# Where the small tables stand in the on-chip memory of a two-block transformer kernel

## The chip, the cores and the metric

The kernel runs on one NeuronCore of a Trainium2 chip. The metric is the device time of one execution in microseconds (us). It was run three times: 1253.51 us in the median, 1253.32 to 1254.24 us in all. A separate execution was recorded by the hardware profiler, and all rows below come from that one.

## The reference, cut to what matters

The program computes two stacks of two layers each on an input `x` of 256 tokens by 1024 features in float32. The first stack has a spatial gating unit beside an RWKV-7 time mix, then dilated attention, each followed by a gated feed-forward layer with a three-tap convolution. The second stack has block attention and a short gated convolution, each followed by a SwiGLU layer, with shifts, scales and gates computed from a condition vector.

```python
for layer in range(DEPTH):                                   # first stack
    x = x + mixer(rmsnorm(x, g)) @ w_out
    x = x + conv_glu_ffn(rmsnorm(x, ff_norm[layer]), w_up, conv_w, conv_b, w_down)
x = rmsnorm(x, final_norm)
for i in range(DEPTH):                                       # second stack
    sh_m, sc_m, g_m, sh_f, sc_f, g_f = split(silu(c) @ w_ada[i] + b_ada[i])
    x = x + g_m * mixer_2(modulate(x, norm_mix[i], sh_m, sc_m))
    x = x + g_f * swiglu(modulate(x, norm_ffn[i], sh_f, sc_f), w_gate_up[i], w_down[i])
```

Nearly all of the arithmetic is in the dense products with weights from DRAM: `w_in`, `w_qkv`, `w_up` and `w_gate_up` (1024 rows), the output matrices (1024 by 1024) and `w_down` (2816 by 1024).

## The kernel before, in words

Every float32 factor of a large product is split into a high part, rounded to the TensorE type fp32r, and a low part, the rounding's remainder. A product is then three matmuls: high by high, high by low, low by high.

**Weights.** `sync_program` loads chunks of 1 or 2 MB from DRAM into two ring buffers (`ring0`, `ring1`, 4096 columns each). Half a chunk at a time, ScalarE makes the high part (`split_hi`, L617) in one of four buffers `WHI`, and VectorE the low part (`split_lo`, L623) in one of four buffers `WLO` (2048 columns each, float32 size). TensorE takes the halves in order and gives each back through the semaphore `w_used`.

**The four kinds of stream on TensorE.** With NK = 8 blocks of 128 rows to sum over:

- `pe_tile` (L1080 to L1082) keeps a 128x128 block of weights in the array and sends 256 columns (the 256 tokens) of the activations `HT0` or `HT1`, three matmuls per block. In the profile `HT0` is `hhi`/`hlo` and `HT1` is `ghi`/`glo`.
- `pe_rows` (L1095 to L1097) and `pe_first` (L847 to L849) do the reverse: a block of the activations is in the array, and 256 columns of `WHI`/`WLO` are sent. In `pe_first` for the feed-forward layers those are two runs of 128 columns, 1024 columns apart; in `pe_rows` one run of 256.
- `pe_sum_part` (L1109) has a block of `YT` (`yhi`/`ylo`) in the array and sends 512 columns of `WHI`/`WLO`.

In every matmul row of the profile the names after the arrow are the operand that is sent and then the one in the array; LDWEIGHTS rows (PEld) are the loading of the latter.

**Places in the memory.** Buffers are handed out in the order of the `sb` and `part` calls, from the bottom of each partition upwards, each at the next free place: first the ring, `WHI`, `WLO`, `X`, `XN` and `YT` (131,072 bytes together in each partition), then the small tables `CT` (constants, 2120 columns), `COL` (776), `MODC` (64), `SM` (192) and `ONE_R32` (128), together 3280 columns or 13,120 bytes, and then `AHI`/`ALO` (2 KB each) and one region that `RW`, `HT0`, `SV` and later `HT1`, `AR`, `GBT`, `ACC` and others use in turn. `TMPS` and the others in an `ExitStack` that is closed at once share their place with what follows.

**Order of the work.** It is written out by hand for each engine (`OD`, `MO`, `walk`, `ADA_AT`, the bank plan for the eight PSUM banks); engines meet only in semaphores. No table of costs looks at an address.

Of the kernel before, what the change touches and what calls it, by code (L numbers as in the profile page):

```python
# [9 lines left out]
F32R = mybir.dt.float32r  # L10
# [28 lines left out]
NC = C_Y64 + 6 * 64  # L39
# [417 lines left out]
def program(nc, A, consts, out):  # L457
    with ExitStack() as ctx:
        def sb(name, cols, dt=F32, rows=128):
            return ctx.enter_context(nc.sbuf_tensor(name, [rows, cols], dt))  # L460
# [4 lines left out]
        def c3(ap, k):  # L465
            return ap.rearrange("p (k n) -> p k n", k=k)
# [4 lines left out]
        def rep(ap, n):  # L471
            return ap.unsqueeze(1).to_broadcast([ap.shape[0], n, ap.shape[1]])
# [10 lines left out]
            return flat(ap)[0].partition_broadcast(128)  # L483


        ring = [sb(f"ring{i}", SLOT) for i in range(NS)]
        WHI = [sb(f"whi{i}", HALF, F32R)[:, :] for i in range(NB)]
        WLO = [sb(f"wlo{i}", HALF, F32R)[:, :] for i in range(NB)]
        X = c3(sb("x", 2 * D)[:, :], 2)
        XN = c3(sb("xn", 2 * D)[:, :], 2)  # L490
        YT = [c3(sb(f"y{i}", NK * T, F32R)[:, :], NK) for i in ("hi", "lo")]
        CT = sb("consts_sb", NC)
        COL = sb("cols", 6 * 128 + 8)
        MODC = sb("modc", 2 * 4 * 8)
        SM = sb("small", 192)
        ONE_R32 = sb("one_r", 128, F32R)[:, :]
        NORM = ExitStack()
        TMPS = [part(NORM, f"tmp{i}", 512)[:, :] for i in range(2)]
        NORM.close()
# [17 lines left out]
        PS = [ctx.enter_context(nc.psum_tensor(f"ps{i}", [128, 512], F32)) for i in range(8)]  # L517
        ident = CT[:, C_ID:C_ID + 128]
        ones = CT[:, C_ONE:C_ONE + 128]

# [9 lines left out]
        def area(kib, n):  # L530
            return AR[:, kib * 256:kib * 256 + n]
# [10 lines left out]
        def ps_of(key):  # L542
            return PS[bank_of[key][0]]

        def bank_sem(key):
            return bank_sems[bank_of[key][0]]
# [131 lines left out]
        def cc(name, i=0, n=1):  # L678
            return COL[:, col[name] + i:col[name] + i + n]

        def conv_col(l, j, i):
            q = l * 3 + j
            s = (1 + q // 2) * 128 + q % 2 * 44 + i
            return COL[:, s:s + 1]

        small_at = [0]

        def sm(n):
            s = small_at[0]
            small_at[0] += n  # L690
            assert small_at[0] <= 192
            return SM[:, s:s + n]

# [60 lines left out]
        def mask(c):  # L754
            return rep(CT[:, c:c + 128].bitcast(U32), 4)

        def mask64(c, n):
            return rep(CT[:, c:c + 64].bitcast(U32), n)

# [4 lines left out]
        GB = [[GBT[:, 1024 * (2 * l + f):1024 * (2 * l + f) + 1024] for f in range(2)] for l in range(2)]  # L764
        modc = MODC[:, :].rearrange("p (l q k) -> p l q k", l=2, q=4)
        AW = c3(area(16, 4096), NK)
# [30 lines left out]
        def pe_column(e, t):  # L797
            ps = opened(e, ("col", t))
            e.wait_ge(S[f"rows{t}"], 16 * len(row_parts[t]))
            k = n_rows[t]  # L800
            e.transpose(ps[:, 0:k], PRS[t][0:k, :], CT[0:k, C_ID:C_ID + k]).then_inc(S["col_turned"], 1)

        COL_ORDER = (6, 0, 1, 2, 3, 4, 5)

        def dve_column(e, t):
            e.wait_ge(S["col_turned"], COL_ORDER.index(t) + 1)
            e.tensor_copy(COL[:, t * 128:t * 128 + n_rows[t]],
                          ps_of(("col", t))[:, 0:n_rows[t]]).then_inc(bank_sem(("col", t)), 1)
# [395 lines left out]
        def sync_program(e):  # L1204
# [8 lines left out]
            for dst, src in ((W2A[0:64, :], A["ev_w2"][0]), (W2A[64:128, :], A["ev_a2"][0]), (G2, A["ev_g2"][0])):  # L1213
                e.dma_start(dst, src).then_inc(S["lora_in"], 16)
            e.dma_start(CT[:, C_ONE:], consts[:, C_ONE:]).then_inc(S["consts_in"], 16)
            w.made = 1
# [113 lines left out]
        def scalar_program(e):  # L1330
# [187 lines left out]

            e.activation(ONE_R32, ones, ACT.Copy).then_inc(S["one_in"], 1)
            act_ffn(e, w, 0, 1, ("u", 1))  # L1520
# [171 lines left out]
        def gate_no(n):  # L1692
            return n // 6 * 2 + n % 2 + 1
# [999 lines left out]
        def pe_ada_sums(e, blocks):  # L2693

            for n in blocks:
# [5 lines left out]
                e.wait_ge(S["ada_lo"], gate_no(n))  # L2701
                e.matmul(ps[:, :], ONE_R32, AHI, start=True, stop=False)
                e.matmul(ps[:, :], ONE_R32, ALO, start=False, stop=True).then_inc(S["ada_mm"], 1)

# [60 lines left out]
```

## Time and profile before

| | |
|---|---|
| median of three runs | 1253.51 us |
| span of the profiled execution | 1253.0 us |
| TensorE busy (PE) | 1230.9 us, 9987 matmuls |
| TensorE weight loads (PEld) | 1147.4 us |
| VectorE busy (DVE) | 933.6 us |
| ScalarE busy (ACT) | 703.9 us |
| mean DMA rate | 211 GB/s |
| mean granted TensorE clock | 0.999 |

The span of the profiled execution is 0.5 us below the median of the runs. A busy TensorE is one that has a matmul somewhere in its pipeline: consecutive matmuls overlap in the record (the one that takes 281 ns is followed by the next after less than half of that), so the distance from start to start, and not the duration of a row, tells how fast a stream goes.

### The profile page before, as it was taken

To read this page: it belongs to the slowest core of one execution; us is meant where nothing else is said; L and a number is where in the kernel's file an instruction comes from. 1 tells how busy PE (TensorE), PEld (TensorE's weight loads), DVE (VectorE), ACT (ScalarE), POOL (GpSimd) and SP (SyncE) were. 2 spreads that over 40 slices of the span, in tenths; PEclk is the share of its full clock that TensorE was granted. 3 is DMA by queue.
4 is the path that set the end of the run, shared out by engine and by line. 5 is a ranking of instruction groups with operands and counts; after the bars stand their busy time and mean duration, and the time that the engine had idled before them with its cause. 6 is when DMAs were issued, how large, how long until landed. Compare 5 with 4: busy or idle time off the path is not lost.

```text
span 1253.0 us, 23639 instructions
## 1 busy us (share of the span) xinstructions
PE 1230.9 (98%) x9987; PEld 1147.4 (92%) x9987; DVE 933.6 (75%) x1260; ACT 703.9 (56%) x1032; POOL 20.1 (2%) x31
## 2 busy tenths in 40 slices
PE   6999999999999999999999999999999999999998
PEld 6999889999999879999988998999998998999997
DVE  5888369888758777999987566899976666677453
ACT  6843477555555767666657556634445554643432
POOL 0002000000000000000000000000000000000000
PEclk9999999999999999999999999999999999999999
DMA  9450277776567256689653534899965356675540
GB/s 322 168 201 4 69 247 246 250 238 229 193 220 257 105 170 234 217 291 319 249 201 119 194 130 148 290 360 351 343 234 202 136 204 200 236 250 188 202 169 34
DMA packets 163683, 263.78 MB, mean 211 GB/s; under 512 B 5677, under 2 KB 98041, under 8 KB 163578
## 3 DMA queue, kind: packets, MB, share of 16 engines
q1 hardware_dynamic: 160586, 259.54, 60.3%
q10 hardware_dynamic: 2992, 2.72, 0.7%
q8 instruction: 79, 1.29, 0.4%
q14 instruction: 26, 0.21, 0.1%
HBM read 261.17 MB, written 1.05 MB: 209 GB/s over the span
## 4 chain that ended last, share of the span: by engine, by line
PE 97%; DVE 1%; ACT 1%; DMA 1%; issue 1%; SPq 0%; DVEq 0%; ACTq 0%
PE ps L1109 26%; PE ps L1080 17%; PE ps L1082 16%; PE ps L1081 16%; PE ps L847 2%; PE ps L848 2%; PE ps L849 2%; PE ps L1095 2%; PE ps L1097 2%; PE ps L1096 2%; PE ps L2397 2%; PE ps L827 1%; DMA ring<-in_ev_w_in_dram 1%; PE ps L2406 1%; PE ps L2597 1%
## 5 line engine op out<-in xcount | busy, mean ns | idle before, releaser
L623 DVE TENSOR_TENSOR wlo<-ring,whi 128x2048 fp32r<-128x2048 f32 x194 | 443.3, 2289 | 97.6 <-ACT whi L617 97.6
L1080 PE MATMUL ps<-ghi,whi 128*128 128x256 f32 x1600 | 449.0, 281 | 0.0
L1081 PE MATMUL ps<-glo,whi 128*128 128x256 f32 x1600 | 446.8, 279 | 0.0
L1082 PE MATMUL ps<-ghi,wlo 128*128 128x256 f32 x1600 | 446.5, 279 | 0.0
L617 ACT ACTIVATE whi<-ring 128x2048 fp32r<-128x2048 f32 x194 | 370.4, 1913 | 96.7 <-PE ps L1109 69.7
L1080 PEld LDWEIGHTS ps<-ghi,whi 128*128 128x128 f32 x1600 | 300.4, 188 | 2.0 <-DVE wlo L623 0.6
L1081 PEld LDWEIGHTS ps<-glo,whi 128*128 128x128 f32 x1600 | 299.7, 187 | 0.8
L1082 PEld LDWEIGHTS ps<-ghi,wlo 128*128 128x128 f32 x1600 | 300.4, 188 | 0.0
L1109 PE MATMUL ps<-whi,yhi 128*128 128x512 f32 x480 | 159.7, 396 | 0.7 <-DVE ylo L1996 0.7
L1109 PE MATMUL ps<-wlo,yhi 128*128 128x512 f32 x480 | 156.7, 390 | 0.0
L1109 PE MATMUL ps<-whi,ylo 128*128 128x512 f32 x480 | 156.6, 390 | 0.0
L1109 PEld LDWEIGHTS ps<-whi,ylo 128*128 128x128 f32 x480 | 90.1, 188 | 19.2
L1109 PEld LDWEIGHTS ps<-wlo,yhi 128*128 128x128 f32 x480 | 90.1, 188 | 18.9
L1109 PEld LDWEIGHTS ps<-whi,yhi 128*128 128x128 f32 x480 | 88.2, 188 | 20.3 <-issue 2.4
L2218 DVE SCALAR_TENSOR_TENSOR acc<-arena,small,acc 128x512 f32<-128x512 f32 x126 | 94.7, 751 | 6.4 <-DMA arena<-in_w_ada_dram 2.5
L2255 DVE SCALAR_TENSOR_TENSOR arena<-arena,cols 128x254 f32<-128x254 f32 (+1 forms) x176 | 73.9, 479 | 14.7 <-ACT arena L1770 14.2
L1774 ACT ACTIVATE arena<-ps 128x256 f32<-128x256 f32 x44 | 16.9, 384 | 111.8 <-PE ps L1082 111.8
L2270 DVE TENSOR_TENSOR ylo<-arena,yhi 128x256 fp32r<-128x256 f32 x88 | 37.1, 422 | 47.6 <-ACT yhi L1787 47.4
L847 PE MATMUL ps<-whi,ghi 128*128 128x256 f32 x224 | 63.5, 283 | 4.0 <-DVE glo L993 4.0
L1768 ACT ACTIVATE arena<-ps 128x512 f32<-128x512 f32 x44 | 26.3, 599 | 67.1 <-PE ps L1082 65.5
L849 PE MATMUL ps<-whi,glo 128*128 128x256 f32 x224 | 62.6, 279 | 0.0
L848 PE MATMUL ps<-wlo,ghi 128*128 128x256 f32 x224 | 62.5, 279 | 0.0
(314 smaller groups left out, 1575.0 us busy)
## 6 DMA issues: line engine op xcount, KB each, us to landing
arena<-in_w_ada_dram SPq DMA_DIRECT2D x48, 1024.0 KB, 6.0
ring<-in_ff_w_up_dram SPq DMA_DIRECT2D x44, 1024.0 KB, 7.6
ring<-in_w_gate_up_dram SPq DMA_DIRECT2D x44, 1024.0 KB, 7.5
ring<-in_ff_w_down_dram SPq DMA_DIRECT2D x10, 2048.0 KB, 7.9
ring<-in_w_down_dram SPq DMA_DIRECT2D x10, 2048.0 KB, 7.8
ring<-in_od_w_qkv_dram SPq DMA_DIRECT2D x6, 2048.0 KB, 8.6
ring<-in_w_qkv_dram SPq DMA_DIRECT2D x6, 2048.0 KB, 7.9
ring<-in_w_in_dram SPq DMA_DIRECT2D x6, 2048.0 KB, 8.1
```

Of the source, the lines that this page charges most:

```text
L617: e.activation(shaped(WHI[i % NB], k), v, ACT.Copy).then_inc(S["w_hi"], 1)
L623: e.tensor_tensor(shaped(WLO[i % NB], k), v, shaped(WHI[i % NB], k).bitcast(F32), ALU.subtract).then_inc(S["w_lo"], 1)
L847: e.matmul(o, h[0][:, c, t], wh, start=c == 0, stop=False)
L848: e.matmul(o, h[0][:, c, t], wl, start=False, stop=False)
L849: x = e.matmul(o, h[1][:, c, t], wh, start=False, stop=c == NK - 1)
L1080: e.matmul(o, wh, h[0][:, k, :], start=k == 0, stop=False)
L1081: e.matmul(o, wh, h[1][:, k, :], start=False, stop=False)
L1082: x = e.matmul(o, wl, h[0][:, k, :], start=False, stop=k == NK - 1)
L1109: x = e.matmul(ps[:, :], YT[l][:, src_k + i, t], w[r][:, i, 512 * h:512 * h + 512], start=first, stop=last)
L2218: e.scalar_tensor_tensor(a, AW[:, k, :], SC[:, k:k + 1], a, ALU.mult, ALU.add).then_inc(S["ada_acc"], 1)
L2255: e.scalar_tensor_tensor(t[a][:, lag:256], z[:, 256 * a:256 * a + 256 - lag], conv_col(f, 2 - lag, a * NF + p), t[a][:, lag:256], ALU.mult ...
L2270: e.tensor_tensor(YT[1][:, p % 8, :], tg[r], YT[0][:, p % 8, :].bitcast(F32), ALU.subtract).then_inc(S["y_lo"], 1)
```

## The change

The five small tables are allocated first, ahead of the ring, and an unused buffer `even` of 16 columns (64 bytes) follows them. All else is as before: the same instructions in the same order, the same semaphores, the same sizes.

```diff
+        CT = sb("consts_sb", NC)
+        COL = sb("cols", 6 * 128 + 8)
+        MODC = sb("modc", 2 * 4 * 8)
+        SM = sb("small", 192)
+        ONE_R32 = sb("one_r", 128, F32R)[:, :]
+        sb("even", 16)
         ring = [sb(f"ring{i}", SLOT) for i in range(NS)]
         WHI = [sb(f"whi{i}", HALF, F32R)[:, :] for i in range(NB)]
         WLO = [sb(f"wlo{i}", HALF, F32R)[:, :] for i in range(NB)]
         X = c3(sb("x", 2 * D)[:, :], 2)
         XN = c3(sb("xn", 2 * D)[:, :], 2)
         YT = [c3(sb(f"y{i}", NK * T, F32R)[:, :], NK) for i in ("hi", "lo")]
-        CT = sb("consts_sb", NC)
-        COL = sb("cols", 6 * 128 + 8)
-        MODC = sb("modc", 2 * 4 * 8)
-        SM = sb("small", 192)
-        ONE_R32 = sb("one_r", 128, F32R)[:, :]
```

The allocator's first free place is byte 1152 of each partition, which 13,120 + 64 bytes of tables and filling bring to 14,336, seven times 2048. So the remainders of the start addresses by 2048 bytes are:

| buffers | before | after |
|---|---|---|
| `ring`, `WHI`, `WLO`, `X`, `XN`, `YT` | 1152 | 0 |
| `CT` | 1152 | 1152 |
| `AHI`, `ALO`, `HT0`, `HT1`, `AR`, `GBT` and the rest | 1984 | 0 |

## Rows read from the trace of the kernel before

**Rows 1.** The page, section 1: busy time of TensorE.

```profile
PE 1230.9 (98%) x9987; PEld 1147.4 (92%) x9987; DVE 933.6 (75%) x1260; ACT 703.9 (56%) x1032; POOL 20.1 (2%) x31
```

**Rows 2.** Waits of TensorE, the longest: who waited for whom, us in total, times, longest.

```profile
PE ps L801 <- DMA pre<-in_ev_norm_dram: 5.1, 1, 5.1
```

**Rows 3.** Groups by line: name, shapes, count | busy us, mean ns | idle before.

```profile
L1080 PE MATMUL ps<-ghi,whi 128*128 128x256 f32 x1600 | 449.0, 281 | 0.0
...
L1109 PE MATMUL ps<-whi,yhi 128*128 128x512 f32 x480 | 159.7, 396 | 0.7 <-DVE ylo L1996 0.7
...
L847 PE MATMUL ps<-whi,ghi 128*128 128x256 f32 x224 | 63.5, 283 | 4.0 <-DVE glo L993 4.0
...
L1095 PE MATMUL ps<-whi,ghi 128*128 128x256 f32 x160 | 45.7, 286 | 0.1
...
L1080 PE MATMUL ps<-hhi,whi 128*128 128x256 f32 x144 | 42.5, 295 | 2.2 <-issue 2.2
...
L1095 PE MATMUL ps<-whi,hhi 128*128 128x256 f32 x32 | 9.1, 286 | 0.0
```

**Rows 4.** Timeline of TensorE, 600 to 604 us (`pe_tile`): start, duration.

```profile
599.85 0.28 PE L1080 MATMUL ps<-ghi,whi 128*128 128x256 f32 x1
...
600.20 0.28 PE L1080 MATMUL ps<-ghi,whi 128*128 128x256 f32 x1
...
600.55 0.28 PE L1080 MATMUL ps<-ghi,whi 128*128 128x256 f32 x1
...
603.73 0.28 PE L1080 MATMUL ps<-ghi,whi 128*128 128x256 f32 x1
```

**Rows 5.** The chain that ended last, 51 to 64 us: start, us, piece.

```profile
51.93 0.12 PE ps L1097
...
62.59 0.11 PE ps L1080
...
62.93 0.44 PE ps L2329 x4
63.37 0.12 PE ps L1080
...
63.72 0.12 PE ps L1080
```

**Rows 6.** Timeline of TensorE, 781 to 785 us (`pe_first`).

```profile
781.23 0.28 PE L847 MATMUL ps<-whi,ghi 128*128 128x256 f32 x1
...
782.25 0.28 PE L847 MATMUL ps<-whi,ghi 128*128 128x256 f32 x1
...
782.95 0.28 PE L847 MATMUL ps<-whi,ghi 128*128 128x256 f32 x1
...
784.72 0.28 PE L847 MATMUL ps<-whi,ghi 128*128 128x256 f32 x1
```

**Rows 7.** The chain, 220 to 227 us (`pe_sum_part`).

```profile
219.90 7.25 PE ps L1109 x32
```

**Rows 8.** Windows: length, busy (count) by engine, granted clock, DMA share, GB/s.

```profile
411.00:413.00 2.00, 2.00 (x20) 2.00 (x19) 1.90 (x5) 0.00 (x0) 0.00 (x0) 1.00 0.00 0
600.00:604.00 4.00, 4.00 (x37) 4.00 (x36) 4.00 (x3) 1.79 (x1) 0.00 (x0) 1.00 1.00 397
697.00:702.00 5.00, 5.00 (x45) 5.00 (x44) 3.47 (x5) 2.33 (x5) 0.00 (x0) 1.00 0.02 5
```

**Rows 9.** The chain, 0 to 60 us: first load, and a product before TensorE speeds up.

```profile
1.65 7.38 DMA ring<-in_ev_w_in_dram
...
20.48 0.21 PE ps L1081
```

**Rows 10.** DMA issues: transfer, queue, count, size, median us to landing.

```profile
arena<-in_w_ada_dram SPq DMA_DIRECT2D x48, 1024.0 KB, 6.0
ring<-in_ff_w_up_dram SPq DMA_DIRECT2D x44, 1024.0 KB, 7.6
```

## The prediction

> **What bounds the kernel now.** The page's busy times come first. TensorE is busy for 1230.9 us of a span of 1253.0 us, VectorE for 933.6 and ScalarE for 703.9 [rows 1]. So TensorE stands still for 22.1 us in all, of which the longest single wait is the 5.1 us before its first instruction, for a small load [rows 2]. No faster load, copy or VectorE operation can be worth more than those 22 us. What else can move the time is the pace of the products themselves, so the second thing to read is which products there are and how far apart they start.
>
> The groups by line give the products of 256 sent columns: each row stands for one of three lines of the same count. They are 3 x (1600 + 144) = 5232 in `pe_tile` and 3 x (224 + 160 + 32) = 1248 in `pe_first` and `pe_rows`, 6480 together. Those of 512 sent columns are 3 x 480 = 1440 [rows 3]. The mean durations there (281, 396 ns) overlap, so the pace has to come from the starts.
>
> - `pe_tile` at 600 us: from 599.85 to 603.73 us lie 33 starts, 117.6 ns each [rows 4].
> - The same line at 52 to 62 us: from 51.93 to 62.59 us lie 94 starts, 113.4 ns each [rows 5].
> - `pe_first` has both in one stream: 9 starts from 781.23 to 782.25 us are 113.3 ns apart, 15 from 782.95 to 784.72 us are 118.0 [rows 6].
> - `pe_sum_part`: 32 in 7.25 us, 226.6 ns each, twice the short pace of 256 columns [rows 7].
>
> So products of 256 columns have exactly two paces, 4.4 ns apart. Going along the timeline I count about 840 at the short pace and 5,600 at the long one (a few are irregular). Nearly all of `pe_tile` goes at the long pace (the short one only around 52 to 63, 87 to 93, 485 and 676 to 682 us), and about half of the 1248 others go at the short one. The total is 6480 x 0.118 + 1440 x 0.227 = 765 + 327 = 1092 us, 87% of the span: this is where an address could count.
>
> **What the change removes, adds and moves.** No instruction, DMA, wait or semaphore is added, removed or reordered on any engine or queue; `even` is never touched. What changes is start addresses. The large operands start at remainder 1152 (the weights, `YT`, ring) or 1984 (`HT0`, `HT1`, arena) of 2048 bytes before, and at 0 after. Each of the following effects is therefore a price per access.
>
> *Crossing a 2 KB boundary.* In `pe_tile` a product sends 1024 bytes starting at 1984 + 1024k. For even k that crosses a multiple of 2048, for odd k it does not. Successive triples of one k start 0.35 us apart in both cases (599.85, 600.20, 600.55) [rows 4]. In the stretch at the short pace 31 triples fit 10.66 us, with no room for a dear and a cheap kind [rows 5]. Aligned, no such product crosses; by these rows that is worth 0, at most the 0.01 us resolution of a row over a triple, and the long averages make it far less.
>
> *The remainder of the sent operand.* At 51.93 us TensorE goes without a pause from sending weights (remainder 128 by 256) to sending `hhi` (remainder 192 by 256), and the pace stays 113 ns. After four small matmuls at 62.93 us the same line with the same `hhi` is at 117 ns (63.37 to 63.72) [rows 5]. In [rows 6] the pace changes in mid-stream, with the operands' remainders unchanged. So before the change the pace is something the pipeline falls into, kept until something disturbs it, and the address of the operand does not choose it. I value this at 0. Its bounds: if alignment chose the short pace for all, 5600 x 4.4 ns = 24.6 us are saved; if it chose the long one for all, 840 x 4.4 ns = 3.7 us are lost, and 6.3 us more if the 512-column products got the same step (1440 x 4.4 ns).
>
> *DMA traffic against TensorE.* The stretch at 411 us goes at the short pace with a DMA share of 0.00, the one at 697 us at the long one with 0.02 (45 products in 5.00 us with those at the edges), the one at 600 us also, with 1.00 [rows 8]. So where DMAs land has no say in the pace: 0.
>
> *DMAs themselves.* In 1.65 to 9.03 us the chain is the first 1 MB of weights [rows 9]; the ring starts off a multiple of 256 bytes and will start on one. The gain is between 0 and 1.4 us: the lower end because nothing about the transfer's pieces changes, the upper because the fastest other 1 MB load lands in 6.0 us and this one took 7.4 [rows 9, 10]. (The 6.0 us load also has longer pieces, so it overstates.) I take 0.2 us, near the lower end, since after this load ScalarE's and VectorE's work for the norm still lies before the first product. All later loads are behind TensorE's work, which is busy for all but 22.1 us.
>
> The Trainium skill, "DMA: Bandwidth & Descriptors", section "How a descriptor splits into AXI transactions", says that a piece which does not start at a multiple of 256 bytes begins with a transfer from the boundary below and pays for the unused bytes. By it a 1 KB piece off the boundary costs up to 36 beats where 32 would do, which of the 7.4 us would be 0.8 (an estimate); it speaks of reads, and the trace has no aligned ring load to test it.
>
> *VectorE and ScalarE.* They read and write the same buffers at new addresses, and are idle for 319 and 549 us [rows 1], so a small change in their pace is hidden. If it weren't, the 22.1 us of TensorE's idle time would grow; I put 0.
>
> Sum: 1253.0 - 0.2 = 1252.8 us for the profiled execution. The runs' median lies 0.5 us above that execution, so the forecast is 1253.3 us.
>
> **The rivals.**
>
> *Long pace gone (faster).* One memory serves both the load of the next block into the array and the columns that are sent; where their addresses stand to one another may decide which of the two paces a stream keeps. For it: every stream at the long pace has `HT0` or `HT1` on one side, whose remainder differs from that of the weights on the other; the 512-column products, whose two operands have the same remainder now, run at 226.6 ns, exactly twice the short pace [rows 7]. The change gives all of them one remainder. Against it: [rows 5, 6], both paces at one pair of addresses; and a 512-column product leaves more time for the load, which may be why it has one pace only. Price 24.6 us: 1228.9 us. If only some streams change over, some 10 to 14 us and 1240 us.
>
> *All overhead gone (much faster).* If what the products take beyond one column per cycle came from misaligned starts, both shapes would gain. Half of the 0.21 us that a product takes at 20.48 us, at the lower clock level [rows 9], is 0.107 us (256 columns at 2.4 GHz). Then 5600 x 10.9 + 880 x 6.7 + 1440 x 13.3 ns = 61 + 6 + 19 = 86 us go: 1167 us. Against it is that the overhead is proportional to the columns (6.7 for 256, 13.3 for 512), where a bad start would cost once.
>
> The Trainium skill, "TensorE: Matmul & The Clock Gate", section "Back-to-back issue gap", gives columns / 2.4 + 2.5 ns: 109.2 and 215.8 ns. No row reaches either; if aligned operands did, the same sum would give some 67 us, 1187 us (an estimate).
>
> *Addresses now coincide (slower).* With all remainders 0, load and sent columns start in the same place of every 2 KB, and if the two sides meet in the same part of the memory each meeting costs. It decides from the point where a stream that now goes at the short pace can no longer keep it. Then those 840 products pay 3.7 us (1257.2 us), and if the 512-column ones, which are in step already, also take the step, 6.3 us more: 1263.5 us. For it: the long pace is by far the commoner one, so it is easily fallen into. Against it: the 512-column products have equal remainders now and do not take the step.
>
> *The change does nothing at all:* 1253.5 us, in the forecast's case.
>
> **How the numbers follow.** Forecast (addresses have no say) 0.50, with its own range 1251.5 to 1254.8 us. Long pace gone 0.20, partly gone 0.07, all overhead gone 0.03. Coinciding addresses 0.20, half of it with the 512-column products. A measurement of this kernel tells about 0.2%, 2.5 us, from no change. So faster 0.30, same 0.50, slower 0.20. The range of 1227 to 1260 us takes in the forecast, both cases of a lost long pace, and the first half of the slower case; outside remain 0.03 below and about 0.10 above.
>
> **What would show it.** If I am right, starts in `pe_tile` stay 117.6 ns apart and in `pe_sum_part` 226.6, the stretches at 113 ns are about as many as now, and busy TensorE stays at 1231 us. If `pe_tile` shows 113.3 ns between starts throughout, the first rival holds; under 113, the second; if `pe_rows` around 411 us shows 118 or `pe_sum_part` over 227, the third. The first ring load landing sooner than 7.4 us, with the first product of the `lora` tile ahead of 15.4 us, would show the DMA term. What makes me wrong is a dependence on addresses that the trace of before, having only one set of them, cannot show.

## The result and the profile after

The changed kernel is slower: 1269.11 us in the median (1268.82 to 1269.93, four runs) against 1253.84 us; the ratio is 1.0122, 95% interval 1.011 to 1.0134. The span of its profiled execution is 1267.0 us, 14.0 us more than before. The forecast was 1253.3 us, and the measured time lies 9 us above the upper end of the stated range, 1260 us.

The page after, section 1, answers to [rows 1]:

```profile
PE 1245.5 (98%) x9987; PEld 1162.7 (92%) x9987; DVE 934.9 (74%) x1260; ACT 703.2 (56%) x1032; POOL 20.7 (2%) x31
```

TensorE is busy 14.6 us longer with the same 9987 matmuls, and its idle time is 21.5 us where it was 22.1. So the loss lies in the pace of the products. All line numbers after the diff are one higher. Here is the timeline of TensorE after, in `pe_tile`, which answers to [rows 4]; columns are start and duration in us:

```profile
606.76 0.28 PE L1081 MATMUL ps<-ghi,whi 128*128 128x256 f32 x1
...
610.72 0.28 PE L1081 MATMUL ps<-ghi,whi 128*128 128x256 f32 x1
```

From 606.76 to 610.72 us lie 33 starts: 120.0 ns each, where it was 117.6. The timeline where `pe_rows` ends and `pe_tile` with `hhi` begins answers to [rows 5]:

```profile
51.82 0.28 PE L1098 MATMUL ps<-whi,hlo 128*128 128x256 f32 x1
51.94 0.28 PE L1081 MATMUL ps<-hhi,whi 128*128 128x256 f32 x1
...
63.10 0.28 PE L1081 MATMUL ps<-hhi,whi 128*128 128x256 f32 x1
```

From 51.94 to 63.10 us: 93 starts, 120.0 ns. It was 113.4. `pe_first` in the third feed-forward layer, which showed both paces in [rows 6], has only 120 ns too:

```profile
789.80 0.28 PE L848 MATMUL ps<-whi,ghi 128*128 128x256 f32 x1
...
790.52 0.28 PE L848 MATMUL ps<-whi,ghi 128*128 128x256 f32 x1
```

(six starts in 0.72 us). The 512-column products are as they were in [rows 7], 24 in 5.44 us, 226.7 ns. This is the chain that ended last, after:

```profile
221.92 5.44 PE ps L1110 x24
```

Summed over all starts (each product is given the time to the next start), the 5232 products of `pe_tile` take 10.9 us more, the 672 of `pe_first` 2.1, the 576 of `pe_rows` 2.9, the 1440 of `pe_sum_part` 0.2 less, and everything else 1.7 less, of which 0.5 us is an earlier start. That is the whole of the 14.0 us. Both old paces, 113.3 and 117.8 ns, are gone and a third one, 120.0 ns, stands in their place. The 0.5 us at the start and the DMA issues answer to [rows 9, 10]:

```profile
1.65 6.92 DMA ring<-in_ev_w_in_dram
```

```profile
arena<-in_w_ada_dram SPq DMA_DIRECT2D x48, 1024.0 KB, 5.5
ring<-in_ff_w_up_dram SPq DMA_DIRECT2D x44, 1024.0 KB, 7.2
```

### The profile page after: what moved, and what is told of

Its sections match the earlier page's. It is cut to its first block, busy times and chain, and to the rows that moved or that the text cites. A ratio compares the mean times of both kernels' runs of the same rounds, so it can differ in the third digit from the quotient of the medians.

```text
span 1267.0 us, 23639 instructions
## 1 busy us (share of the span) xinstructions
PE 1245.5 (98%) x9987; PEld 1162.7 (92%) x9987; DVE 934.9 (74%) x1260; ACT 703.2 (56%) x1032; POOL 20.7 (2%) x31
## 3 DMA queue, kind: packets, MB, share of 16 engines
q10 hardware_dynamic: 2992, 2.72, 0.8%
## 4 chain that ended last, share of the span: by engine, by line
PE 97%; DVE 1%; ACT 1%; DMA 1%; issue 1%; SPq 0%; DVEq 0%; ACTq 0%
PE ps L1110 25%; PE ps L1081 17%; PE ps L1082 17%; PE ps L1083 17%; PE ps L848 2%; PE ps L850 2%; PE ps L849 2%; PE ps L1096 2%; PE ps L1098 2%; PE ps L1097 2%; PE ps L2398 2%; PE ps L828 1%; DMA ring<-in_ev_w_in_dram 1%; PE ps L2407 1%; PE ps L2598 1%
## 5 line engine op out<-in xcount | busy, mean ns | idle before, releaser
L624 DVE TENSOR_TENSOR wlo<-ring,whi 128x2048 fp32r<-128x2048 f32 x194 | 443.1, 2288 | 100.2 <-ACT whi L618 99.9
L1081 PE MATMUL ps<-ghi,whi 128*128 128x256 f32 x1600 | 454.1, 284 | 0.0
L1083 PE MATMUL ps<-ghi,wlo 128*128 128x256 f32 x1600 | 452.7, 283 | 0.0
L1082 PE MATMUL ps<-glo,whi 128*128 128x256 f32 x1600 | 452.7, 283 | 0.0
L1081 PEld LDWEIGHTS ps<-ghi,whi 128*128 128x128 f32 x1600 | 306.8, 192 | 2.0 <-issue 1.2
L1082 PEld LDWEIGHTS ps<-glo,whi 128*128 128x128 f32 x1600 | 306.9, 192 | 0.9
L1083 PEld LDWEIGHTS ps<-ghi,wlo 128*128 128x128 f32 x1600 | 306.8, 192 | 0.0
```

Source lines behind the costliest of these rows:

```text
L624: e.tensor_tensor(shaped(WLO[i % NB], k), v, shaped(WHI[i % NB], k).bitcast(F32), ALU.subtract).then_inc(S["w_lo"], 1)
L1081: e.matmul(o, wh, h[0][:, k, :], start=k == 0, stop=False)
L1082: e.matmul(o, wh, h[1][:, k, :], start=False, stop=False)
L1083: x = e.matmul(o, wl, h[0][:, k, :], start=False, stop=k == NK - 1)
```

## The experiments

In all of them no instruction changes, only the places of buffers. `sb` counts columns of 4 bytes, so 48 columns are 192 bytes. "Mean pace" is worked out from all starts between 105 and 130 ns apart (for `pe_sum_part`, under 245 ns). The difference D is the start of `HT0`/`HT1` minus the start of the weights, in bytes modulo 256.

**1. Is it the boundary or the relative position?**

```diff
-        sb("even", 16)                    # e1_no_even: all at remainder 1984, D = 0
```

> The tables stay in front, the 64-byte filling is left out: weights, YT and HT0/HT1 all start at remainder 1984 by 2048 bytes, so they are still equal to one another but at no boundary. Theory 1 (what counts is how the addresses of the two operands stand to one another): all products of 256 columns start 120.0 ns apart as after the change, about 1269 us. Theory 2 (what counts is that operands start on the 2 KB boundary): 113 and 118 ns as before the change, about 1254 us.

```diff
+        sb("even", 16)                    # e2_acts_aligned: kernel before, behind the tables; D = 128
```

> The order of before, with only the 64-byte filling behind the tables: weights and YT at remainder 1152, HT0/HT1 and the arena at 0 (896 bytes ahead by 1024). Theory 1 (relative position): not 120 ns throughout; a pace of its own, since this difference is a new one. Theory 2a (HT on the 2 KB boundary is what costs): 120 ns, 1269 us.

```diff
         YT = [c3(sb(f"y{i}", NK * T, F32R)[:, :], NK) for i in ("hi", "lo")]
+        sb("gap", 240)                    # e3_gap960: 960 bytes, D = 192
+        sb("gap", 80)                     # e4_gap320: instead, 320 bytes, D = 64
```

> The kernel after with 960 unused bytes between YT and the rest: weights at 0, HT0/HT1 at 960. Theory 1 (relative position): not 120 ns, near 113 to 118, under 1262 us. Theory 2b (weights on the 2 KB boundary are what costs): 120 ns throughout, 1269 us.

> The kernel after with 320 unused bytes between YT and the rest: weights at 0, HT0/HT1 at 320. Before the change HT stood 832 bytes behind the weights by 2048, which is 320 by 512. Theory 1, if the pattern repeats every 512 bytes or less: the two paces of before, 113.3 and 117.8 ns, with pe_tile nearly all at the longer, about 1254 us. Theory 2b (weights on the boundary cost): 120 ns, 1269 us.

Measured against before: without `even` 1270.23 us, ratio 1.0139 (1.011 to 1.0169); HT aligned alone 1265.62 us, 1.0103 (1.0073 to 1.0132); gap 960 1246.04 us, 0.9934 (0.9906 to 0.9962); gap 320 1253.56 us, 1.0003 (0.9991 to 1.0014). The timeline of the kernel without `even`, in which no large operand starts on a 2 KB boundary:

```profile
606.98 0.28 PE L1080 MATMUL ps<-ghi,whi 128*128 128x256 f32 x1
...
609.86 0.28 PE L1080 MATMUL ps<-ghi,whi 128*128 128x256 f32 x1
```

24 starts in 2.88 us are 120.0 ns. The boundary is not it. With weights on the boundary and a gap of 960, the page and the `pe_tile` pace at 598 us are these:

```profile
PE 1222.3 (98%) x9987; PEld 1139.5 (92%) x9987; DVE 933.1 (75%) x1260; ACT 704.2 (57%) x1032; POOL 20.3 (2%) x31
```

```profile
597.75 0.28 PE L1082 MATMUL ps<-ghi,whi 128*128 128x256 f32 x1
...
599.87 0.28 PE L1082 MATMUL ps<-ghi,whi 128*128 128x256 f32 x1
```

Here 18 starts in 2.12 us are 117.8 ns; over the whole kernel about half of the `pe_tile` streams run so and half at 113.3. TensorE is busy 23.2 us less than after the change. Both rival theories, that the weights or the activations on a boundary cost, are out: each was on one in a kernel without the uniform 120.0 ns (the activations in the second, whose mean was 119.3). And gap 320 gives back the paces of before, D = 64 as there (1984 - 1152 = 832 = 3 x 256 + 64). Nor is it the place of one operand by itself, modulo 256. The activations start at 192 both without `even` (119.9 ns in the mean) and with the gap of 960 (115.8), and the weights start at 0 both after the change (119.9) and with the gap of 960 (115.8). Only the difference tells them apart.

**2. How often does the pattern repeat, and how fine is it?** The same diff with other gaps.

> The kernel after with 512 unused bytes between YT and the rest: HT0/HT1 stand 512 bytes ahead of the weights by 2048. If the relative position counts and its pattern repeats every 512 bytes: 120.0 ns throughout, 1269 us, as with difference 0. If it repeats only every 1024: another pace. If only equality counts (difference exactly 0 by 2048): 113 to 118 ns, about 1250 us.

> 256 unused bytes between YT and the rest. If the pattern repeats every 256 bytes: 120.0 ns throughout, 1269 us. If every 512: a pace of its own; with 0 at 120 ns and 320 at 117.5, and half a period between the two operands, I expect the cheapest of all, 113.3 ns, about 1240 us.

> 128 unused bytes between YT and the rest. If the pattern repeats every 128 bytes: 120.0 ns, 1269 us. If every 512 and it is symmetric about 0, this equals a difference of 384, which gave a mixture around 119.3 ns and 1265 us.

> 64 unused bytes between YT and the rest. If the pattern repeats every 64 bytes 120.0 ns, 1269 us (that is already spoken against by 320 and 960). If it is symmetric about 0 with a period of 512, this equals 448, which 960 gave: 115.8 ns in pe_tile, about 1246 us.

> 224 unused bytes between YT and the rest. So far, by the difference HT minus weights modulo 256: 0 gives 120.0 ns in pe_tile, 64 117.5, 128 119.3, 192 115.8. If the memory is told apart in steps of 64 bytes only, an HT that starts at 32 past such a step lies between its neighbours 192 and 0: 116 to 120 ns, 1246 to 1269 us. If finer steps count, it may be below 115.8 ns, down to 113.3 (some 1232 us).

> 160 unused bytes between YT and the rest. In steps of 64 bytes it lies between 128 and 192: 116 to 119 ns in pe_tile. If finer steps count, it may be below 115.8 ns.

> 208 unused bytes between YT and the rest, 16 beyond the best so far. If only steps of 64 bytes count, as 192: 115.8 ns in pe_tile, 1243 to 1246 us. If steps of 16 count, another pace than 192.

> 32 unused bytes between YT and the rest. In steps of 64 bytes between 0 and 64: 117.5 to 120 ns in pe_tile, 1253 to 1269 us. If a difference of exactly 0 is the dear case, 117.5 ns at most.

| gap, bytes | D | us, median | ratio to before (95%) | mean pace `pe_tile` | `pe_first`, `pe_rows` |
|---|---|---|---|---|---|
| 0 (the change) | 0 | 1269.11 | 1.0122 (1.011 to 1.0134) | 119.9 | 119.8 |
| 256 | 0 | 1268.84 | 1.0111 (1.0081 to 1.014) | 119.9 | 119.8 |
| 512 | 0 | 1269.17 | 1.0113 (1.0084 to 1.0143) | 119.9 | 119.8 |
| 32 | 32 | 1251.88 | 0.9982 (0.9971 to 0.9993) | 116.8 | 118.3 |
| 64 | 64 | 1252.79 | 0.9985 (0.9974 to 0.9997) | 117.5 | 116.3 |
| 320 | 64 | 1253.56 | 1.0003 (0.9991 to 1.0014) | 117.5 | 116.2 |
| 128 | 128 | 1264.23 | 1.0074 (1.0045 to 1.0103) | 119.3 | 118.8 |
| 160 | 160 | 1260.13 | 1.0045 (1.0029 to 1.0062) | 118.1 | 119.8 |
| 960 | 192 | 1246.04 | 0.9934 (0.9906 to 0.9962) | 115.8 | 117.0 |
| 208 | 208 | 1257.59 | 1.0028 (1.0016 to 1.0039) | 118.3 | 117.0 |
| 224 | 224 | 1257.1 | 1.0026 (1.0015 to 1.0038) | 118.3 | 116.8 |

Before the change, D = 64, the means are 117.6 and 115.5. The pattern repeats every 256 bytes: 0, 256 and 512 agree to 0.03% and 64 and 320 to 0.06%. HT aligned alone, D = 128, had 119.3 and 118.9, as the gap of 128 has. My guesses of a symmetric pattern (64 as 960, 256 as the best) and of a pace under 115.8 ns between the steps fell. So did the guess that only steps of 64 bytes count: 16 bytes more than 192 bring `pe_tile` from 115.8 to 118.3 ns, and a gap of 32 gives 116.8, which is below both of its neighbours, 119.9 at 0 and 117.5 at 64. 208 and 224 give one pace.

Taken as sent minus loaded operand, D is what the table says for `pe_tile` and its negative for `pe_first` and `pe_rows`, whose roles are exchanged. With that, 192 beats 64 in both: 115.8 against 117.5 in `pe_tile`, and in `pe_rows` alone 115.0 (gap 64) against 116.3 (gap 960). The table holds a sharper test of this exchange of roles. A gap of 32 gives 116.8 in `pe_tile` and 118.3 in the other two; a gap of 224, which is 32 with the roles exchanged, gives 118.3 and 116.8. So what counts is the sent operand's start minus the loaded one's, whichever of them holds the weights.

**3. Whose positions are they?**

```diff
+        sb("gap1", 48)                    # h1_ht1_only: 192 bytes before HT1
         HT1 = [c3(part(ctx, f"g{i}", NK * T, F32R)[:, :], NK) for i in ("hi", "lo")]
+        sb("gap2", 16)                    # and 64 behind it
```

> The kernel after, HT1 alone moved: 192 unused bytes before HT1 and 64 behind it, so that HT0, the arena, gates and accumulators stay at multiples of 256 and only ghi/glo stand 192 ahead of the weights. Theory 1 (the pace comes from the sent operand against the one being loaded): streams with ghi/glo as with 960, 115.8 ns in pe_tile, streams with hhi/hlo still at 120.0; about 1247 us. Rival (the other engines' accesses to the arena and the rest make it): 120.0 ns for all, 1269 us.

In `h2_glo_only`, `gap1` stands between `ghi` and `glo` instead.

> The kernel after with only glo moved by 192 bytes; ghi stays level with the weights. One product in three sends glo (while a block of WLO is loaded), the other two send ghi (while WHI is loaded). Theory 1: a price per meeting of a pair, so only the product with glo gets cheaper: a mean between 115.8 and 120 ns, some 118.5, 1262 us. If the stream as a whole locks in: either 120.0 or 115.8 throughout.

HT1 alone: 1246.46 us, ratio 0.994 (0.9912 to 0.9969), as with the gap of 960. In this one kernel the timeline shows `hhi`, which did not move, at 120 ns, and `ghi`, which did, at the long pace of 117.8 (in other streams at 113.3; the mean of its `pe_tile` products is 115.9):

```profile
52.86 0.28 PE L1083 MATMUL ps<-hhi,whi 128*128 128x256 f32 x1
...
55.74 0.28 PE L1083 MATMUL ps<-hhi,whi 128*128 128x256 f32 x1
...
596.08 0.28 PE L1083 MATMUL ps<-ghi,whi 128*128 128x256 f32 x1
...
597.84 0.28 PE L1083 MATMUL ps<-ghi,whi 128*128 128x256 f32 x1
```

24 starts in 2.88 us against 15 in 1.76 (117.3). The arena, gates and accumulators moved by 256 bytes and so kept their places modulo 256; what the other engines do there has no part in it. `glo` alone: 1257.23 us, 1.0022 (1.001 to 1.0033), mean 118.0 in `pe_tile`. That is a mean between the two, as the price per pair would have it; but the gaps inside a triple vary, so no pair can be given its own price.

**4. Do the 512-column products have a price too?**

```diff
+        sb("gap1", 48)                    # h3_yt192 (b1_yt192): YT and HT 192 ahead of the weights
         YT = [c3(sb(f"y{i}", NK * T, F32R)[:, :], NK) for i in ("hi", "lo")]
```

In `h4_yt64` `gap1` has 64 bytes, and 128 more follow YT. `b2_yt0` has 192 bytes behind YT and none before.

> The kernel after with 192 unused bytes before YT, so YT as well as HT0/HT1 and the rest stand 192 ahead of the weights. Theory: the two readers meet at a price of 6.67 ns (113.33 is 106.67 plus one such step, 120.0 plus two, 226.67 is 213.33 plus two), and the relative position sets how often. If so, pe_sum_part, in which the weights are sent and YT loaded, may lose a step: 220.0 instead of 226.67 ns, 9.6 us over 1440 products, about 1236 us. If a product of 512 columns always meets the load twice: 226.67 as before, about 1246 us.

> The kernel after with 64 unused bytes before YT and 128 behind it: YT 64 ahead of the weights, HT0/HT1 192 ahead. In pe_sum_part the weights are the sent side, so 64 here is what 192 is in pe_tile. If the relative position counts for 512 columns too, this is the better of the two for them: 220.0 ns, about 1236 us. If not: 226.67 ns, about 1246 us.

> The kernel after with 192 unused bytes before YT (YT, HT0/HT1 and all behind them 192 ahead of the weights), timed in five rounds. Theory 1: about 1241 us, 1.0% faster than before the change, with pe_tile at 114.8 ns and pe_sum_part at 229.1. If the one look was a lucky one: as b2_yt0.

> The same with the 192 bytes behind YT, so that YT stays level with the weights and only HT0/HT1 and the rest are 192 ahead; by 256 this is the same as the gap of 960. Theory 1 (only the remainder by 256 counts): as the gap of 960, 1246 us, pe_tile 115.8 ns, pe_sum_part 227.3. If larger strides count too: another time.

YT at 192: 1241.51 us, 0.99 (0.9848 to 0.9952), and measured again, in six executions, 1237.6 us, 0.9874 (0.9854 to 0.9894). YT at 64: 1247.16 us, 0.9939 (0.9921 to 0.9956). YT level, six executions: 1246.07 us, 0.9927 (0.991 to 0.9944). The expected 220.0 ns never came. The chains that ended last, first of YT at 64, then of YT at 192, then of the gap of 960 (YT level):

```profile
217.97 7.70 PE ps L1112 x33
```

```profile
217.90 5.72 PE ps L1111 x25
```

```profile
217.98 8.16 PE ps L1111 x36
```

That is 233.3, 228.8 and 226.7 ns: here a difference of 0 is the best of the three. The gain comes in `pe_tile`, whose mean falls to 114.5 (YT at 64), 114.8 and 113.9 (YT at 192, `h3_yt192` and `b1_yt192`) from 115.4 to 115.8 (YT level). With YT at 64 the wide products take it back: they cost 7.9 us more than with YT level. The page and the timeline of the best kernel:

```profile
PE 1212.9 (98%) x9987; PEld 1127.7 (91%) x9987; DVE 932.4 (75%) x1260; ACT 705.1 (57%) x1032; POOL 20.4 (2%) x31
```

```profile
590.59 0.28 PE L1082 MATMUL ps<-ghi,whi 128*128 128x256 f32 x1
...
593.99 0.28 PE L1082 MATMUL ps<-ghi,whi 128*128 128x256 f32 x1
```

30 starts in 3.40 us, 113.3 ns. At one set of addresses a stream still falls into one of two paces. Of the 218 stretches of 24 products in `pe_tile` 9 run at the short one in the kernel before, 99 with the gap of 960, and 198 in the best.

The traces show how YT, which `pe_tile` does not touch, has a say in this: through the beginning of a stream. Fourteen times a `pe_tile` stream begins directly behind `pe_sum_part`. With YT level (before, `e3_gap960`, `b2_yt0`) all 14 settle at 117.8 ns. With YT at 192 all 14 settle at 113.3 in `b1_yt192` and 13 of 14 in `h3_yt192`, and with YT at 64 3 of 14 do. A stretch that follows another one directly keeps its pace, in 170 of 171 cases in the kernel before (the other comes right behind the first stretch, which goes at 213 ns, the lower clock level) and in all 171 in the best. Here is the same stream of the best kernel (24 starts in 2.72 us, 113.3 ns) and of `b2_yt0` (24 in 2.82, 117.5 to the resolution of the rows), which differ in the place of YT alone:

```profile
224.17 0.28 PE L1082 MATMUL ps<-ghi,whi 128*128 128x256 f32 x1
...
226.89 0.28 PE L1082 MATMUL ps<-ghi,whi 128*128 128x256 f32 x1
```

```profile
224.44 0.28 PE L1082 MATMUL ps<-ghi,whi 128*128 128x256 f32 x1
...
227.26 0.28 PE L1082 MATMUL ps<-ghi,whi 128*128 128x256 f32 x1
```

It also accounts for a spread between executions of one kernel. `h3_yt192` and `b1_yt192` have the same places; their profiled executions differ by 6.4 us in span and by 6.1 us in `pe_tile`, with 151 and 198 stretches at the short pace.

## Why the prediction was wrong

- *What bounds the kernel:* right. The whole difference is in the distance of TensorE's starts, at an unchanged idle time.
- *Crossing a 2 KB boundary, 0:* right. Levels with and without crossings have the same 120.0 ns if D = 0.
- *DMA traffic against TensorE, VectorE and ScalarE, 0:* right; the duration of the largest VectorE operation went from 2289 to 2288 ns.
- *DMAs themselves, 0.2 us:* the sign was right, the size less than half of what was measured: 7.38 to 6.92 us, and TensorE's first tile 0.5 us earlier. The first load varies by as much between the experiments (6.76 to 7.44 us with the ring at a multiple of 256 bytes). The median over 44 loads is steadier: 7.5 or 7.6 us in the three kernels whose ring starts off a multiple of 256 bytes, 7.1 to 7.3 us in all others. The Trainium skill's rule ("DMA: Bandwidth & Descriptors", "How a descriptor splits into AXI transactions") speaks of reads and points the same way; my estimate of 0.8 us from it was too high, since the median fell by 0.4 us.
- *The remainder of the sent operand, 0:* this step failed. I wrote that "the address of the operand does not choose it". [Rows 5, 6] do show two paces at one pair of addresses. But the trace held only two differences of sent operand minus loaded one, 64 (`pe_tile`) and 192 (`pe_first`, `pe_rows`, where the roles are exchanged), and both allow both paces. A difference of 0 or 128 did not occur in these 6480 products. From "addresses do not choose between the two" I concluded "addresses have no say", and took the two paces seen as the bounds. The true value was outside both: 120.0 ns for all, 15.9 us over the 6480 products. The bound of 3.7 us for the loss rested on the 117.8 ns as the worst there is.
- *The rival "addresses now coincide":* this one named what counts, the place of the two operands relative to one another, with a chance of 0.20 and the wrong price; that the two reads meet in the memory is not shown. It put 840 products up to 117.8 ns and perhaps 4.4 ns on the 1440 wide ones: 1257 to 1263.5 us. Measured were steps of 2.2 ns from the long pace and 6.7 ns from the short one (17.2 us over the 6390 products whose starts are regular; at the 90 irregular ones 1.3 us came back), and nothing on the wide ones, whose difference stayed 0. My evidence against it, that the 512-column products have equal remainders and are not slow, did not carry over: equal is the best for them and the worst for 256 columns.
- *The counts:* by stretches of 24, 38 of 270 (912 products) went at the short pace, where I counted 840 and, for the rival "all overhead gone", used 880. By 912 the largest loss that I allowed for in this step is 4.0 us and not 3.7.
- *The rival "long pace gone":* it can be had for most of `pe_tile`, but by keeping the operands apart, by 192 bytes, and not by levelling them: 99 of the 218 stretches with the gap of 960, 198 with YT at 192 too.

The Trainium skill, "TensorE: Matmul & The Clock Gate", section "Step-by-step: what each phase is for", says: "Loading the next tile's weights doesn't steal SBUF read bandwidth from the running matmul." By that rule moving HT1 alone would change nothing. It moved the `pe_tile` products that send `ghi` and `glo` from 120.0 to 115.9 ns. So for fp32r operands with a load before each product the two reads are not independent of one another, and the measurement decides.

## What to carry to other kernels

When a stream of matmuls with a new load before each one runs within a few per cent of its floor, look at where the sent and the loaded operand start relative to one another, modulo 256 bytes, and time three or four differences (one `sb` filler each). Aligning everything to a large power of two is the layout in which they are equal, here the worst for 256 columns. Look at the wide streams too: the place of their operands can set the pace of the stream behind them. And a trace bounds a cost only for the configurations that occur in it: list which are missing before calling a parameter harmless.

## What the runs showed of the hardware

- Products of 256 fp32r columns with a load of 128x128 each start 113.3 or 117.8 ns apart at D = 64 or 192, and 120.0 ns, after the first few starts of a stream, at D = 0. 120.0 - 113.3 is 6.7 ns, 16 columns (64 bytes) at 2.4 GHz. A meeting of the two readers in one of four 64-byte parts of every 256 bytes would fit the period and this price. That is argued, not shown, and it leaves open why a difference of 128 costs nearly as much as 0 (119.3 against 119.9 ns) and why 208 differs from 192 (118.3 against 115.8).
- Products of 512 columns take 226.7 ns with YT level with the weights, 228.8 with YT at 192 and 233.3 with YT at 64.
- A stream settles at one of its two paces within its first few starts and keeps it; which one depends on what ran before it. Behind the 512-column products it was 117.8 ns in 14 of 14 cases with YT level and 113.3 in 14 of 14 (in a second execution 13) with YT at 192.
- A 1 MB load of 2 KB pieces into the arena takes 5.3 to 5.5 us in four kernels with ring and arena at multiples of 256 bytes, but 6.8 us in the fifth such kernel (`h2_glo_only`). With the arena elsewhere it takes 5.6 to 6.4 us, and 6.2 us where the arena was on and the ring off such a multiple. So an effect of the arena's place on its loads is not shown.
- Open: by what means the products before a stream put it into one of its two paces, whether matmuls of other types see the period of 256 bytes, and whether `YT` at other differences would give both fast wide products and the short pace.
